# First up slab of a layer by token tile, from reused attention memory, and modulation sums in another order

## The chip, the core and the metric

The kernel runs on one core of a Trainium2 chip. The metric is the device time of one execution in microseconds; lower is better. All data is float32. TensorE runs at one of two clocks, and the profile gives the granted one as a share of 2.4 GHz.

## The reference, cut to what matters

Two blocks follow each other on 256 tokens of width 1024. The first has an even layer (Fourier mix and latent attention) and an odd layer (grouped attention), which also carry 256 context tokens. The second has two hybrid layers:

```python
u = layer_norm(x) * (1 + sc1) + sh1
proj = u @ w_in + b_in                # pool, conv, two attentions, 4 x 1024 gates
for n in range(4): merged += sigmoid(gate[n]) * (branch[n] @ w_branch[n])
x = layer_norm(ALPHA * x + g1 * (merged @ w_o)) * ln1_g + ln1_b
u2 = layer_norm(x) * (1 + sc2) + sh2
hdn = square(relu(u2 @ w_up + b_up))  # 1024 -> 4096
x = layer_norm(ALPHA * x + g2 * (hdn @ w_down)) * ln2_g + ln2_b
```

The shifts, scales and gates (`sh1`, `sc1`, `g1`, ...) are products of `silu(c)` with a 1024-wide matrix each, plus a bias.

## The kernel before

**Matmuls.** A float32 product at full precision is three products of parts: a weight slab (128 x 2048, 1 MB) is copied by ScalarE to a rounded high part (`high`, L1562, 1.9 us) and VectorE subtracts it from the slab for the low part (`low`, L2137, 2.3 us). The activations are split in the same way (`split_u`, L2449 and L2450). All matmuls are recorded at line 766, transposes at line 926.

**Slabs.** The SP queue loads the slabs in one fixed order, LAYER_SLABS, into `weight_ring` with three slots; a slab waits for its slot to be free. A slot comes free when VectorE has made the low part, or, for a `branch` slab, which is not split, when TensorE has used it. The high and low parts have two slots each; they come free when TensorE has used them. A gate tile of a hybrid layer takes two `gate` halves and one `branch` slab, so exactly the ring.

**Modulation.** A modulation vector is a weighted sum of matrix rows: POOL issues 1 MB chunks into `modulation_ring` (two slots, L638), VectorE adds each with a scalar (`gemv`, L1979, two instructions of 1.28 us for each stream; vectors 2 to 4 of the first block have two streams, latent and context, 5 and later one), and TensorE adds the 128 partial sums by a product with ones (`reduce_part`). Chunk q of vector c can be issued when VectorE has used the chunk two before it.

**Gate tile g of a hybrid layer.** TensorE: the features of gate g (96 matmuls of 256 columns), then branch g. ScalarE's queue: split of gate g+1, both halves, then tanh of gate g, which frees gate g's banks. These are the banks of gate g+1. VectorE: low parts of gate g+1, the products of gate and branch, then two chunks of gemv. POOL adds to `mergedT`.

**From the output projection to the MLP.** `o0` is computed for both token tiles at once, `o1` tile by tile. VectorE adds the residual and takes statistics (`halves_of_tile`, L2084 to L2091), centres and scales (`centred`, `scaled`, L2606 and L2612), takes statistics of the result (`statistics_again`) and writes the normalised tile `xn` (`normal`, L2120); POOL gives the inverse roots (L666). TensorE turns a tile of `xn` when it is ready (`turn_xn`) and computes the sums of vectors 1, 2 and 3 and some `keep_busy` matmuls between. ScalarE modulates the turned `xn` (L1838), VectorE splits it in four blocks, and only then does `up0` start, by features with all 256 tokens in each matmul (96 matmuls of 256 columns). `up0` is an ordinary slab of the ring. Then `up1`, `down0`, `up2` and so on.

**Memory.** Tensors share addresses by phase. Where the hybrid layer's attention keeps `qT`, `kT`, `v`, `prob` and where the pool matrices and forget sums lie, nothing is live from the fifth gate tile on; the last two of these places are those of the MLP's `hidden_high` and `hidden_low`.

**Even layer.** VectorE's order around the Fourier mix: split of `kva`, gemv (3,1), statistics of `qa` and `kva` with one `mgate` split between, the other `mgate` split, gemv (3,2), the four Fourier products (L2225), gemv (3,3), (4,0), (4,1), the gated tiles of `mgate`, rotations. TensorE's Fourier step g+1 (`f2`) writes the one bank that product g frees, and `mgate` follows step 3.

## Time and profile before

| what | value |
|---|---|
| median of 3 runs | 1394.52 us (1393.18 to 1396.90) |
| profiled execution | 1396.87 us, of it span 1395.10 |
| mean granted clock of TensorE | 0.983 |
| busy: TensorE, weight loads, VectorE, ScalarE, POOL | 94%, 78%, 68%, 36%, 11% |
| HBM read | 255.49 MB, 184 GB/s over the span |

Busy time says little by itself: TensorE's 94% count its filler matmuls too. What matters is where TensorE waits, for whom, and what that engine did before. Even and odd layer take the first 500 us or so, each hybrid layer some 450.

### The profile page before, as it was taken

Reading aid. Unit: us, or ns where it says so; the run is one execution under the profiler, and the core shown is the slowest. Engines: PE = TensorE matmul, PEld = TensorE weight load, DVE = VectorE, ACT = ScalarE, POOL = GpSimd, SP = SyncE. Lnnn points to the kernel's source line nnn. Section 1 sums busy time; section 2 is a strip of 40 time slices with the busy share of each in tenths; the row PEclk is TensorE's granted clock in tenths of the full one; section 3 lists DMA queues with packets and bytes.
Section 4 is the critical chain, followed back from the end, with each engine's and each line's share of the span. In section 5 each row is a group of like instructions: output and inputs, shape, how many; then the busy total and the mean of one; then the engine's idle time right before and its main releaser. Section 6 shows DMA issues by size and latency. Waiting matters only on the chain.

```text
span 1395.1 us, 19034 instructions
## 1 busy us (share of the span) xinstructions
PE 1314.8 (94%) x7923; PEld 1085.6 (78%) x7923; DVE 950.1 (68%) x1221; ACT 499.6 (36%) x769; POOL 151.3 (11%) x168
## 2 busy tenths in 40 slices
PE   5997999999999899999998999998999999999996
PEld 3796855446875459899887889886988998889895
DVE  4866667557488567577788666657667778755546
ACT  3321135214246023543323344323354333343432
POOL 2201100100000010012222000001001231100000
PEclk9998999999999999999999999999999999999998
DMA  9653360225420465577774777545656785455551
GB/s 358 232 178 108 138 211 1 95 87 183 157 100 1 153 214 184 197 257 270 273 286 142 235 245 246 182 151 181 200 187 247 260 299 199 136 192 186 181 181 61
DMA packets 104911, 257.77 MB, mean 185 GB/s; under 512 B 8213, under 2 KB 11766, under 8 KB 104570
## 3 DMA queue, kind: packets, MB, share of 16 engines
q1 hardware_dynamic: 80432, 171.75, 36.1%
q0 software_dynamic: 20192, 75.58, 15.0%
q10 hardware_dynamic: 4202, 9.23, 1.9%
q8 instruction: 63, 1.03, 0.3%
q14 instruction: 22, 0.18, 0.0%
HBM read 255.49 MB, written 1.05 MB: 184 GB/s over the span
## 4 chain that ended last, share of the span: by engine, by line
PE 70%; DVE 17%; DMA 4%; ACT 4%; issue 4%; POOL 1%; ACTq 0%; POOLq 0%; SPq 0%; DVEq 0%
PE bank L766 68%; DVE weights_low L2137 2%; PE bank L926 2%; DMA weight_ring<-in_w_in_dram 2%; DMA start_ring<-in_w_mod_dram 1%; DVE modulation_sums L1979 1%; ACT odd_prob L1751 1%; DVE statistics L2091 1%; POOL inverse_roots L666 1%; DVE negated_maxima L2381 1%; ACT weights_high L1562 1%; DMA modulation_ring<-in_w_mod_dram 1%; DMA modulation_ring<-in_w_ada_dram 1%; ACT even_A L1696 1%; DVE x L2090 1%
## 5 line engine op out<-in xcount | busy, mean ns | idle before, releaser
L2137 DVE TENSOR_TENSOR weights_low<-weight_ring,weights_high 128x2048 fp32r<-128x2048 f32 (+1 forms) x124 | 272.5, 2200 | 223.4 <-ACT weights_high L1562 223.3
L1562 ACT ACTIVATE weights_high<-weight_ring 128x2048 fp32r<-128x2048 f32 (+1 forms) x124 | 227.5, 1837 | 390.2 <-PE bank L766 315.5
L766 PE MATMUL bank<-uT_high,weights_high 128*128 128x256 f32 (+1 forms) x1200 | 342.0, 285 | 6.0 <-issue 2.7
L766 PE MATMUL bank<-uT_low,weights_high 128*128 128x256 f32 (+1 forms) x1200 | 340.1, 283 | 0.0
L766 PE MATMUL bank<-uT_high,weights_low 128*128 128x256 f32 (+1 forms) x1200 | 340.0, 283 | 0.0
L766 PEld LDWEIGHTS bank<-uT_high,weights_high 128*128 128x128 f32 (+1 forms) x1200 | 228.8, 191 | 11.3 <-ACT gate_tanh L1892 6.2
L766 PEld LDWEIGHTS bank<-uT_low,weights_high 128*128 128x128 f32 (+1 forms) x1200 | 228.9, 191 | 1.1
L766 PEld LDWEIGHTS bank<-uT_high,weights_low 128*128 128x128 f32 (+1 forms) x1200 | 228.8, 191 | 0.5
L1979 DVE SCALAR_TENSOR_TENSOR modulation_sums<-modulation_ring,silu_c_columns,modulation_sums 128x1024 f32<-128x1024 f32 x112 | 148.7, 1327 | 21.8 <-DMA modulation_sums<-in_b_ada_dram 7.1
L766 PE MATMUL bank<-weights_high,hidden_high 128*128 128x512 f32 x256 | 102.7, 401 | 1.2 <-DVE weights_low L2137 1.2
L766 PE MATMUL bank<-weights_low,hidden_high 128*128 128x512 f32 x256 | 102.0, 398 | 0.0
L766 PE MATMUL bank<-weights_high,hidden_low 128*128 128x512 f32 x256 | 102.0, 398 | 0.0
L638 POOL DMA_DIRECT2D modulation_ring<-in_w_ada_dram x48 | 34.7, 724 | 520.9 <-DVE modulation_sums L1979 511.0
L666 POOL TENSOR_TENSOR inverse_roots<-newton,inverse_roots 128x1 f32<-128x1 f32 (+1 forms) x25 | 25.6, 1023 | 412.7 <-DVE newton L2102 332.7
L766 PE MATMUL bank<-x,weight_ring 128*128 128x256 f32 x256 | 58.0, 380 | 2.0 <-issue 2.0
L766 PEld LDWEIGHTS bank<-weights_high,hidden_high 128*128 128x128 f32 x256 | 48.8, 191 | 12.5 <-issue 1.6
L766 PE MATMUL bank<-weight_ring,even_yT 128*128 128x512 f32 x128 | 55.7, 594 | 2.5 <-DVE even_yT L2279 1.4
L766 PEld LDWEIGHTS bank<-weights_high,hidden_low 128*128 128x128 f32 x256 | 48.6, 190 | 11.8
L766 PEld LDWEIGHTS bank<-weights_low,hidden_high 128*128 128x128 f32 x256 | 48.7, 190 | 10.9
L766 PE MATMUL bank<-weights_high,uT_high 128*128 128x256 f32 (+1 forms) x160 | 53.4, 334 | 1.8 <-DVE uT_low L2450 1.2
L766 PEld LDWEIGHTS bank<-x,weight_ring 128*128 128x128 f32 x256 | 47.5, 190 | 8.5 <-issue 2.8
L766 PE MATMUL bank<-weights_high,uT_low 128*128 128x256 f32 (+1 forms) x160 | 52.2, 327 | 0.0
(311 smaller groups left out, 2184.6 us busy)
## 6 DMA issues: line engine op xcount, KB each, us to landing
weight_ring<-in_w_in_dram SPq DMA_DIRECT2D x52, 1024.0 KB, 6.4
modulation_ring<-in_w_ada_dram POOLq DMA_DIRECT2D x48, 1024.0 KB, 6.9
weight_ring<-in_w_up_dram SPq DMA_DIRECT2D x32, 1024.0 KB, 5.4
weight_ring<-in_w_down_dram SPq DMA_DIRECT2D x32, 1024.0 KB, 4.9
modulation_ring<-in_w_mod_dram POOLq DMA_DIRECT2D x16, 1024.0 KB, 5.8
weight_ring<-in_o_w_in_dram SPq DMA_DIRECT2D x10, 1024.0 KB, 5.2
weight_ring<-in_w_branch_dram SPq DMA_DIRECT2D x16, 512.0 KB, 3.7
weight_ring<-in_w_o_dram SPq DMA_DIRECT2D x8, 1024.0 KB, 6.9
```

Source lines behind the costliest of these rows:

```text
L638: pool.dma_start(mring[:, slot, :].rearrange("p (k n) -> p k n", k=2), w.rearrange("(k p) n -> p k n", p=P)[:, 2 * q:2 * q + 2, c0:c0 + D] ...
L666: pool.tensor_tensor(root[:, 0, c:c + n], nwt[:, 0, c:c + n], root[:, 1, c:c + n], ALU.pow).then_inc(S["root_ready"], 1)
L766: return track(pe.matmul(*args, **kw))
L926: return track(pe.transpose(o, src, ident[0:rows, 0:rows]))
L1562: act.activation(ring[:, s, c0:kn * cols], wring[:, slot, c0:kn * cols], ACT.Copy).then_inc(S["high_ready"], 1)
L1696: ins = act.activation(prob_e[:, b, c0:c0 + n], src, ACT.Exp, bias=negmax[:, b, i:i + 1], accum_out=esum[:, b, i:i + 1])
L1751: ins = act.activation(oprob[:, b, j, i, :], o[:, :], ACT.Exp, bias=negmax[:, b, n:n + 1], accum_out=esum[:, b, n:n + 1])
L1979: ins = dve.scalar_tensor_tensor(out=a, in0=w[:, k, :], scalar=ccol[:, col:col + 1], in1=a, op0=ALU.mult, op1=ALU.add)
L2090: link(dve.scalar_tensor_tensor(out=xc, in0=xc, scalar=scale, in1=tmp, op0=ALU.mult, op1=ALU.add))
L2091: return dve.bn_stats(stat[:, i, 6 * h:6 * h + 6], xc)
L2137: dve.tensor_tensor(lo[:, s, c0:kn * cols], wring[:, slot, c0:kn * cols], hi[:, s, c0:kn * cols].bitcast(F32), ALU.subtract).then_inc(w_fr ...
L2381: ins = dve.tensor_reduce(m[:, i:i + 1], ready(("OS", p, i, j))[:, :], AX_X, ALU.max, negate=True)
```

## The change

It does three things. (a) `up0` leaves the ring's order. Its two halves are loaded by the SP queue ahead of `gate6` into memory that the attention no longer needs, are split there by ScalarE and VectorE in gate tiles 5 and 6 (`high_late`, `low_late`), the low part over the raw one. The other slabs move up in the ring. (b) `up0` is computed by token tile: the turned and modulated tile 0 is multiplied as soon as it is split (24 matmuls of 512 columns for each tile), each result is copied by ScalarE to `gate_tanh`'s memory, turned by TensorE (four transposes a tile) and goes on as before. VectorE's residual steps stand in another order for that, and the `keep_busy` calls between the modulation sums fall from ten to two. In layer 0 gemv (4,1) moves behind the split of `down0`. (c) On VectorE and POOL the gemv blocks of the first block stand in another order: (3,1) and (3,2) behind the Fourier products, (4,0) and (4,1) behind the first rotations, (5,0) and (5,1) behind the even attention, (6,0) and (6,1) behind the last `og` split.

```diff
                + [s for j in range(8) for s in halves(f"gate{j}") + [(f"branch{j}", 0)]]
-               + halves("o0", "o1", "up0") + [s for j in range(1, 8) for s in halves(f"up{j}", f"down{j - 1}")]
+               + halves("o0", "o1") + [s for j in range(1, 8) for s in halves(f"up{j}", f"down{j - 1}")]
...
-    jobs += mod_jobs(LAYER_MODS, 1, lo) + mod_jobs(LAYER_MODS, 2, lo)
-    jobs += [(("x2T", i), hi) for i in range(4)] + mod_jobs(LAYER_MODS, 3, lo)
+    jobs += mod_jobs(LAYER_MODS, 1, (4,)) + mod_jobs(LAYER_MODS, 2, (5,))
+    jobs += [(("x2T", t, b), (4 + 2 * t + b,)) for t in range(TC) for b in range(2)] + mod_jobs(LAYER_MODS, 3, lo)
+    jobs += [(("upt", t), (4 + t,)) for t in range(TC)]
...
                 for name, h in LAYER_SLABS:
+                    if (name, h) == ("gate6", 0):
+                        b, n = sec.bank(("PV", 3), 1)
+                        sp.wait_ge(free[b], n)
+                        for part in range(2):
+                            sp.dma_start(up_raw[part].rearrange("p (k n) -> p k n", k=4),
+                                         w_slab("up0", part, l)[0]).then_inc(late_in[part], 16)
...
-            mod_chunks(sec, 3)
+            mod_chunks(sec, 3, 0, 1)
             inverse_root(2, 0, TALL)
             inverse_root(3, 0, TALL)
+            mod_chunks(sec, 3, 2, 3)
             mod_part(sec, 4)
             mod_part(sec, 5)
             mod_chunks(sec, 6, 0, 1)
             mod_start(sec, 6)
-            mod_chunks(sec, 6, 2, 3)
             for i in range(TALL):
                 inverse_root(4 + i, i)
+            mod_chunks(sec, 6, 2, 3)
             mod_part(sec, 7)
 
...
+                if name == "up0":
+
+                    pe.wait_ge(S["late_low"], sec.at("late_low", h + 1))
+                    return [v.rearrange("p (k n) -> p k n", k=4) for v in up_parts[h]]
...
                 reduce_part(1)
-                keep_busy(start(("x2T", 0)), 3)
                 reduce_part(2)
-                keep_busy(start(("x2T", 0)), 3)
-                turn_xn("x2T", TC, between=lambda: reduce_part(3))
-                keep_busy(start(("up", 0, 0)), 4)
+                keep_busy(start(("x2T", 0, 0)), 2)
+                turn_tile(0, "x2T", TC)
+                reduce_part(3)
+                def up_of_tile(o, tt, ks):
+
+                    for k in ks:
+                        if k % 4 == 0:
+                            pe.wait_ge(S["u_ready"], sec.at("u_ready", 8 + 2 * tt + k // 4 + 1))
+                        ins = multiply(o[:, :], ui(k, tt), cut(slab("up0", k // 4), k % 4, 0, COLS),
+                                       start=(k == 0), stop=(k == KD - 1))
+                    if KD - 1 in ks:
+                        done(ins, ("upt", tt))
+
+                def turn_up(outs, tt):
+
+                    copied(("upt", tt))
+                    for i, o in enumerate(outs):
+                        for m in range(2):
+                            ins = turn(o[:, N * m + P * tt:N * m + P * tt + P],
+                                       tanhg[:, tt, P * (2 * i + m):P * (2 * i + m) + P], P)
+                        if tt == TC - 1:
+                            done(ins, ("up", 0, i))
+
+                o = start(("upt", 0))
+                up_of_tile(o, 0, range(6))
+                turn_tile(1, "x2T", TC)
+                up_of_tile(o, 0, range(6, KD))
+                o = start(("upt", 1))
+                up_of_tile(o, 1, range(4))
+                firsts_up = [start(("up", 0, i)) for i in range(2)]
+                turn_up(firsts_up, 0)
+                up_of_tile(o, 1, range(4, KD))
+
+                def finish_first(k):
+
+                    if k == 3:
+                        turn_up(firsts_up, 1)
+
                 for j in range(9):
-                    if j < 8:
+                    if 1 <= j < 8:
                         features_out(both(f"up{j}"), [("up", j, 0), ("up", j, 1)], u, N, 2,
-                                     wait=u_split(2) if j == 0 else lambda k: None)
+                                     wait=finish_first if j == 1 else lambda k: None)
                     if j == 8 and not sec.last:
...
 
+                def high_late(h):
+
+                    act.wait_ge(late_in[h], l * 16 + 16)
...
                                 ins = act.activation(prob[:, j, c:c + n], o[:, c:c + n], ACT.Exp,
                                                      bias=negmax[:, j, i:i + 1], accum_out=esum[:, j, i:i + 1])
                             release(ins, ("S", g, j))
+                    if g in (5, 6):
+                        high_late(g - 5)
                     if g < 7:
                         high(f"gate{g + 1}")
                         gate_tanh(g)
...
-                high("o1", "up0")
-
+                high("o1", "up1")
+                copied(("mod", 1))
+                copied(("mod", 2))
+                modulate_tile("x2T", 0, mcol2)
+                copied(("o", 1, 1))
+                gate_rows(3, [grow1])
                 act.wait_ge(S["norm1"], sec.at("norm1", 1))
                 load_norm(l, 2)
-                copied(("mod", 1))
-                copied(("mod", 2))
-                modulate_u("x2T", mcol2)
-                gate_rows(3, [grow1])
+                modulate_tile("x2T", 1, mcol2)
+                for tt in range(TC):
+                    copy_out(("upt", tt), tanhg[:, tt, :], ready(("upt", tt))[:, :])
                 for j in range(8):
-                    high(f"down{j - 1}" if j > 0 else "up1")
+                    if j > 0:
+                        high(f"down{j - 1}")
...
             low_e("kva", 1)
-            gemv(3, 1)
 
...
             low_e("mgate", 1)
-            gemv(3, 2)
             copied(("f0",))
...
                 release(ins, ("f2", g))
-            gemv(3, 3)
+            for q in range(1, 4):
+                gemv(3, q)
             mod_columns(2, mcol, 0)
-            for q in range(2):
-                gemv(4, q)
             for m in range(4):
                 gated_tile(("mgate", m), 4 + m, eyT[:, 4 + m, :], tanh_e[:, m % 2, :])
...
                 link(rotate(src, src, cos16[:, i, :], sin16[:, i, :], 1, 16, ps))
+            for q in range(2):
+                gemv(4, q)
             for h in range(2):
...
             ins.then_inc(S["kpe_ready"], 1)
             for q in range(2, 4):
                 gemv(4, q)
-            for q in range(2):
-                gemv(5, q)
             for h in range(MH):
...
-            for q in range(2, 4):
+            for q in range(4):
                 gemv(5, q)
-            for q in range(2):
-                gemv(6, q)
             for v in range(2):
                 copied(("mod", 4, v, 1))
...
             low("og1")
-            for q in range(2, 4):
+            for q in range(4):
                 gemv(6, q)
...
+                def low_late(h):
+
+                    hi, lo = up_parts[h]
+                    dve.wait_ge(S["late_high"], sec.at("late_high", h + 1))
+                    dve.tensor_tensor(lo, up_raw[h], hi.bitcast(F32), ALU.subtract).then_inc(S["late_low"], 1)
...
+                    if g in (5, 6):
+                        low_late(g - 5)
                     if g < 7:
                         low(f"gate{g + 1}")
...
-                low("o1")
+                low("o1", 0)
...
                 def residual_of_mixed(m):
 
+                    link(halves_of_tile("o", 1, 0))
                     link(halves_of_tile("o", 0, 1))
                     variance(0, False, LN_EPS)
                     centred(0)
-                    link(halves_of_tile("o", 1, 1))
-                    variance(1, False, LN_EPS)
                     link(scaled(0, m))
                     statistics_again(0)
-                    centred(1)
-                    normal(0, m + 2)
-                    scaled(1, m + 1).then_inc(S["norm1"], 1)
-                    dve.wait_ge(S["norm1"], sec.at("norm1", 1))
-                    statistics_again(1)
+                    link(halves_of_tile("o", 1, 1))
                     mod_columns(1, mcol2, 0)
                     mod_columns(2, mcol2, 1)
+                    normal(0, m + 1)
+                    variance(1, False, LN_EPS)
+                    centred(1)
+                    scaled(1, m + 2).then_inc(S["norm1"], 1)
+                    dve.wait_ge(S["norm1"], sec.at("norm1", 1))
+                    split_block("x2T", 0, 0)
+                    statistics_again(1)
+                    split_block("x2T", 0, 1)
                     normal(1, m + 3)
 
...
-                for i in range(TC):
-                    link(halves_of_tile("o", i, 0))
+                link(halves_of_tile("o", 0, 0))
+                low("o1", 1)
                 dve.wait_ge(ln_in, l * 64 + 32)
                 residual_of_mixed(1)
-                low("up0", 0)
-                for i in range(4):
-                    copied(("x2T", i))
-                    split_u(i)
-                low("up0", 1)
+                for b in range(2):
+                    split_block("x2T", 1, b)
+                low("up1")
                 for j in range(8):
-                    if not sec.last:
+                    if not sec.last and j != 1:
                         gemv(4 + j // 4, j % 4)
-                    low(f"down{j - 1}" if j > 0 else "up1")
+                    if j > 0:
+                        low(f"down{j - 1}")
+                    if not sec.last and j == 1:
+                        gemv(4, 1)
                     copied(("up", j, 1))
```

`split_block` is the split of four 128 x 128 blocks of one token tile; `copied` waits until a bank is free, `link` for the instruction just issued. `modulate_tile` is the former loop over `xT` with a name, and `turn_tile` the former one of the same name.

## Rows read from the trace of the kernel before

**Rows 1.** the page's chain that ended last, share of the span by engine
```profile
PE 70%; DVE 17%; DMA 4%; ACT 4%; issue 4%; POOL 1%; ACTq 0%; POOLq 0%; SPq 0%; DVEq 0%
```
**Rows 2.** TensorE's timeline, even layer: start, us, instruction, [idle before <- releaser]
```profile
112.21 0.36 PE L766 MATMUL bank<-even_C,even_constants 128*128 128x8 f32 x2 [1.09 <-DVE even_E L2215]
128.68 4.45 PE L766 MATMUL bank<-even_constants,even_C 128*128 128x256 f32 x16 [6.49 <-DVE even_yT L2225]
136.32 1.97 PE L766 MATMUL bank<-even_constants,even_C 128*128 128x256 f32 x8 [1.06 <-DVE even_yT L2225]
...
203.81 0.64 PE L926 MATMUL bank<-constants,even_B 128*96 128x128 f32 x4 [0.49 <-DVE even_E L2263]
```
**Rows 3.** VectorE's timeline in the same stretch, columns as in Rows 2
```profile
106.06 0.57 DVE L2003 BATCH_NORM_STATS2 statistics<-bank 128x6 f32<-128x384 f32 x1
122.62 1.28 DVE L1979 SCALAR_TENSOR_TENSOR modulation_sums<-modulation_ring,silu_c_columns,modulation_sums 128x1024 f32<-128x1024 f32 x1
```
**Rows 4.** windows: length, PE, PEld, DVE, ACT, POOL busy, granted clock, DMA share, GB/s
```profile
128.00:132.00 4.00, 3.32 (x8) 2.70 (x9) 0.53 (x2) 0.00 (x0) 1.78 (x3) 0.51 0.00 0
164.00:168.00 4.00, 4.00 (x19) 3.54 (x20) 1.53 (x14) 1.47 (x3) 1.46 (x2) 0.50 0.28 113
```
**Rows 5.** odd layer, VectorE, then TensorE; landings of chunks issued at 264.4, 267.1
```profile
385.74 5.24 DVE L1979 SCALAR_TENSOR_TENSOR modulation_sums<-modulation_ring,silu_c_columns,modulation_sums 128x1024 f32<-128x1024 f32 x4
394.23 0.68 DVE L2372 COPY odd_kT<-bank 128x512 f32<-128x512 f32 x1
...
395.12 1.99 PE L766 MATMUL bank<-odd_kT,odd_qT 64*128 64x512 f32 x8 [1.36 <-issue]
...
DMA to landing us min/median/max: 5.6/5.6/5.6
...
DMA to landing us min/median/max: 6.5/6.5/6.5
```
**Rows 6.** layer 0, gates 5 and 6: chain of waits, then ScalarE, then TensorE
```profile
665.75 11.68 DMA weight_ring<-in_w_in_dram
...
671.60 1.92 ACT L1562 ACTIVATE weights_high<-weight_ring 128x2048 fp32r<-128x2048 f32 x1 [7.27 <-DMA weight_ring<-in_w_in_dram]
677.45 1.92 ACT L1562 ACTIVATE weights_high<-weight_ring 128x2048 fp32r<-128x2048 f32 x1 [3.92 <-DMA weight_ring<-in_w_in_dram]
...
680.91 0.36 PE L766 MATMUL bank<-uT_high,weights_high 128*128 128x256 f32 x1 [1.27 <-ACT gate_tanh L1892]
```
**Rows 7.** SP queue, landings (branch 5, gate 6, layer 1), one window
```profile
665.23 1.02 SPq L596 DMA_DIRECT2D weight_ring<-in_w_in_dram  x2
...
DMA to landing us min/median/max: 3.6/3.6/3.6
...
DMA to landing us min/median/max: 6.3/9.0/11.7
...
DMA to landing us min/median/max: 6.7/8.6/10.6
...
674.00:678.00 4.00, 4.00 (x29) 3.77 (x28) 1.92 (x1) 0.56 (x1) 0.32 (x1) 1.00 1.03 410
```
**Rows 8.** TensorE's timeline, layer 0, from output projection to MLP
```profile
734.70 1.84 PE L766 MATMUL bank<-constants,modulation_sums 128*128 128x1 f32 x16
...
743.73 1.06 PE L926 MATMUL bank<-constants,xn 128*128 128x128 f32 x8 [2.70 <-DVE xn L2120]
748.66 1.09 PE L926 MATMUL bank<-constants,xn 128*128 128x128 f32 x8 [2.15 <-DVE xn L2120]
...
752.50 0.77 PE L766 MATMUL bank<-uT_high,weights_high 128*128 128x256 f32 x1
...
777.25 0.47 PE L766 MATMUL bank<-weights_high,hidden_high 128*128 128x512 f32 x1 [1.06 <-DVE weights_low L2137]
```
**Rows 9.** VectorE's timeline in the same stretch
```profile
731.74 0.69 DVE L2084 TENSOR_TENSOR xn<-bank,gate_row 128x512 f32<-128x512 f32 x1
...
742.77 0.81 DVE L2120 TENSOR_SCALAR xn<-x,mean_variance,inverse_roots 128x1024 f32<-128x1024 f32 x1 [0.52 <-POOL inverse_roots L666]
```

80 lines of the change are left out of this document (38 added, 42 removed).

## The prediction

> **What bounds the kernel now.** I read the page first: TensorE carries 70% of the chain that ended last [rows 1]. So time is won or lost only where TensorE stands still, runs at its lower clock, or does filler matmuls. Next I read TensorE's timeline at the three places that the change touches; the reader is to see there how long the idle time is and what ended it. They are the last stretch of the even layer's Fourier mix (6.49 us) [rows 2], the hand-over from the output projection to the MLP in each hybrid layer [rows 8, 9], and, as a place that is full today, the gate tiles [rows 6]. Last come the queues beside them: VectorE [rows 3, 5], ScalarE and the SP queue [rows 6, 7].
>
> **Even layer, the gain.** Two gemv blocks (4 instructions of 1.28 us, 5.0 us a block) leave VectorE's path to the Fourier products: one before the statistics of `qa`, one after the last `mgate` split [rows 3]. Without the first, statistics start at 101.1 instead of 106.06 and `qa`'s banks are free near 107.6, so `f0` follows `kva` directly: its 1.09 us wait goes [rows 2], some 1.2 with the restart. TensorE then reaches the point of the long wait at 122.18 - 1.2 = 121.0. The `kva` statistics wait for `kva`'s last tile (111.1) and end with a root near 113.5; the copies and the last split end near 117.9, so VectorE's first product is out before 121.0 and the 6.49 us wait is gone. From 128.68 to `mgate`'s start at 137.94 it is 9.26 us today; 1.35 of them are the first product at the lower clock, which the idle time had brought (0.51 of full) [rows 2, 4]. So `mgate` starts at 121.0 + 7.9 = 128.9, 9.0 us earlier. gemv (3,1) to (3,3) then run 130 to 147, beside `mgate` (96 matmuls of 512 columns, some 22.5 us), and end before their sum is wanted at 151. Given back: gemv (4,0) and (4,1), 10.0 us, now stand ahead of the `qb` rotations (157.6 to 167.6), and the second half of `qb` needs those banks: 170.1 against 169.2, 0.9 us. Won: the 0.49 us wait in the key transposes, as gemv (5,0), (5,1) have left that place [rows 2]. Sum **-8.5 us**. It holds through the even attention, where no gemv stands. The four blocks of gate 1's sum behind the attention cost nothing: the output tiles, which come next on VectorE, end later on TensorE. On POOL the latents' roots now go ahead of chunks (3,2) and (3,3), as the second needs gemv (3,1), and those of the odd norm ahead of (6,2); none waits for more than before.
>
> **Odd layer, the price.** gemv (6,0) and (6,1) move behind the last `og` split, so four blocks stand where two stand: today 5.24 us from 385.74, then the four gated tiles and the key copy, which ends at 394.91 and lets the first score matmul go at 395.12 [rows 5]. The move costs more than two blocks of 2.62. The ring has two slots, so POOL can issue chunk (6,2) only when gemv (6,0) has ended: 385.74 + 2.62 + 0.3 = 388.65, and a chunk lands 5.6 us after its issue, its follower 6.5 [rows 5]. gemv (6,2) runs 394.3 to 396.9; (6,3), issued at 391.3, lands at 397.8 and ends at 400.4. Gated tiles and key copy start 9.4 us later than at 391.02, and I take +9.0 for the scores. TensorE stands idle some 8 us, and 6.49 us was enough to bring the lower clock (1.2 of 2.4 GHz) and keep it for 3.3 us of the restart, 128.68 to 132 [rows 2, 4]; half of that, **+1.7**, comes on top. Sum **+10.7**. The blocks can't slide forward: they stand behind the last split, which ends as they begin.
>
> **Hybrid layers, the price.** Three gate slabs fill the three ring slots, so a branch load waits until TensorE has used the last branch, and the SP queue issues branch 5, gate 6 half 0 and half 1 in one burst from 664.82 to 666.25 [rows 7]. ScalarE waits for both halves, 7.27 and 3.92 us [rows 6], and its queue has `high("gate6")` before `gate_tanh(5)`, and the tanh frees the banks that gate 6 needs. The chain of waits runs through that very load (11.68 us) [rows 6]. The change issues `up0`'s two megabytes between branch 5 and gate 6: the wait written there (PV 3's bank) was met at 656, so it delays nothing and protects nothing. Within the SP queue loads land in turn (3.6, 6.3, 11.7 us after issue) [rows 7]. 2.10 MB at the 410 GB/s that both queues move there [rows 7] are 5.1 us; at the rate between branch 5's and half 0's landing, 1.05 MB in 3.15 us, they are 6.3; and the SP queue shares with a modulation chunk for longer. I take +6.4: gate 6's half 1 lands near 683.8, is split 1.92 us, tanh, and TensorE starts 3.5 us after the landing as now, at 687.3 against 680.91 [rows 6]. In layer 1 the half lands 10.6 us after its issue at 1116.0 [rows 7], at 1126.6, just as TensorE frees the buffer, so 1133.0 + 3.5 against 1130.45 without a wait for it: +6.1. I take **+6.25** a layer; the lower end is 3.7 (5.1 less the 1.4 us for which the last modulation chunk may give way), the upper 7.7. Below zero is excluded, as no load gets earlier. TensorE idles 6.6 to 7.7 us, so **+1.7** for the lower clock, as above. ScalarE's extra 1.92 and VectorE's 2.29 us in gates 5 and 6 lie in their waits for the same loads, and cost nothing while those last; without them VectorE has about 1 us to spare in a gate tile. A rule of the Trainium skill bears on this step. The page "DMA: Bandwidth & Descriptors", section "Where 436 GB/s comes from", has transfers from HBM bound at about 358 GB/s; the trace here shows more, 410, so the measurement decides. By the page the two megabytes would take 5.9 us and the layer would lose half a microsecond less; the sum does not use it.
>
> **Hybrid layers, the gain.** Today: `o1` ends and the sums follow at 734.70, residual and statistics of tile 0 on VectorE, turn of tile 0 at 743.73, tile 1 at 748.66, `up0` at 752.50, and `up0` with `up1` (192 matmuls) ends at 776.19 [rows 8]. In the new order VectorE takes tile 1's half 0 at 727.4, tile 0's half 1 at 729.6 (2.2 us earlier), and tile 0's scaling and statistics before tile 1's last half [rows 9]; normal 0 starts at 739.3 against 742.77. (The terms: tile 1's last half 2.2 us as today, POOL's root 1.5, a scaling 1.3, statistics 1.8.) `u` of tile 0's first four blocks is ready near 744.8. Each tile has 24 matmuls of 512 columns, at 0.23 us, twice the 0.12 of today's 192 of 256 columns: 18 of them run before tile 1 is turned (749.5), the rest after, and tile 1's split on VectorE (1.1 us a block) is ready at 752.1 and 753.2. ScalarE's copies of the two sums lie beside TensorE's next blocks. Tile 1 ends at 758.0. Then `up1`, with four transposes in it (0.5 us), ends at 770.2: 6.0 us earlier. The next wait, 1.06 us for a split of `down0` [rows 8], grows to about 1.4, since gemv (4,1) now follows that split. Layer 1 is faster today by 1.1 us (normal 1 took 0.81, not 1.41), so 5.2 there. Two waits inside are short of filler now: only two `keep_busy` calls remain of ten, and the sums of one column each bring the lower clock by themselves [rows 4]; I take 0.6 off. **-4.9** a layer, bounds -3.5 (lower clock throughout `up0`'s first 18 matmuls) and -5.8.
>
> **The sum.** Even -8.5, odd +10.7, two layers of +6.25 + 1.7 - 4.9 = +3.05, so +6.1: together **+8.3 us**. Against the profiled execution, 1396.87 (span 1395.10 and 1.77 around it), that is 1405.2; the median of the runs is 1394.52, so I forecast **1402.8**.
>
> **Rivals.** (1) *The collision is covered*: gate 6's loads land as before, because the DMA engines take them beside `up0` and what stands behind gives way, and the layers keep only their gain: 2 x -4.9 + 2.2 = -7.6, 1386.9. For it: no row shows more than three loads waiting in this queue. Against: the landings in it come in turn [rows 7], and `up0` stands ahead. It decides from the point where half 1 lands before 677. (2) *Half collision*: the stall is 3 us a layer and too short for much of the lower clock (0.8): 2 x -1.1 + 2.2 = 0, 1394.5. (3) *The odd layer's wait is smaller*, chunks landing early: half of 10.7 gone, 1397.5; the landings of 5.6 and 6.5 us speak against it. (4) *The change doesn't do what it says*: `up0` by tile starts at the lower clock and later, saving 1.5 a layer: 8.3 + 6.8 = 1409.6. For it: the idle steps without filler.
>
> **How the numbers follow.** Forecast 0.55 (its own range 1397 to 1409), (1) 0.16, (2) 0.12, (3) 0.1, (4) 0.07. The range reaches from 1388 to 1409: above (1)'s centre, where less than 0.15 is left out, and up to the bounds of the stalls. A measurement of this kernel can tell about 0.3% (4.2 us) from no change. Faster than 1390.3: (1) and a tail of (2), 0.19. Within: the rest of (2), (3)'s lower half, 0.21. Slower: 0.60.
>
> **What would show it.** In the profile after: the score matmuls of the odd layer start after an idle time of about 8 us on TensorE (1.36 before), with POOL's chunk landing ahead of a gemv. Gate 6 starts after a wait of 7 us or so for `gate_tanh`, in both layers, with ScalarE waiting for the weight ring. `mgate` starts near 129. `up1` ends 35.5 us after `o1` in layer 0, against 41.5. The forecast is wrong if gate 6 starts within 2 us of branch 5's end, if VectorE does not wait between gemv (6,1) and (6,2), or if the Fourier stage keeps a wait of over 3 us.

## The result, and the profile of the changed kernel

| kernel | median | ratio to before, 95% interval | span of the profiled execution | mean granted clock |
|---|---|---|---|---|
| before | 1394.19 us (1393.18 to 1396.90, 4 runs) | | 1395.1 us | 0.983 |
| after | 1409.54 us (1408.66 to 1411.22, 4 runs) | 1.0108 [1.0094, 1.0122] | 1409.4 us | 0.976 |

Ratios are taken against executions of the kernel before made beside each run, whose medians were 1394.2 to 1395.3 us; one execution of e6 (3308.79 us) and one of the kernel before (3321.88 us) are left out of them.

The change costs 15.4 us by the medians and 14.3 us in the two profiled spans. The forecast had the sign right and the size wrong: 8.3 us, 1402.8, and the time lies above the range's end of 1409. The page of the changed kernel: its span, the granted clock in tenths over 40 slices, and the engines' shares of the chain that ended last. Before, that chain held 4% of DMA [rows 1]; now it holds 7%.

```profile
span 1409.4 us, 18841 instructions
...
PEclk9999999999989999999899999999999989999999
...
PE 69%; DVE 14%; DMA 7%; ACT 4%; issue 4%; POOL 1%; ACTq 1%; SPq 0%; POOLq 0%; DVEq 0%
```

To find where the time went, take TensorE's timeline in both kernels, note when the same matmul starts, and subtract. Each stage's own cost is the step from one line to the next.

| TensorE starts | before | after | later by | forecast |
|---|---|---|---|---|
| even output projection | 259.92 | 250.71 | -9.2 | -8.5 |
| odd scores | 395.12 | 394.91 | -0.2 | +0.5 |
| hybrid layer 0 | 500.88 | 502.14 | +1.3 | +2.2 |
| layer 0, branch 5 | 676.02 | 677.89 | +1.9 | +2.2 |
| layer 0, gate 6 | 680.91 | 690.71 | +9.8 | +8.5 |
| layer 0, branch 6 | 692.50 | 705.00 | +12.5 | +10.2 |
| layer 0, sums behind `o1` | 734.70 | 747.31 | +12.6 | +10.2 |
| layer 0, `up2` | 788.51 | 797.01 | +8.5 | +5.3 |
| hybrid layer 1 | 950.23 | 956.06 | +5.8 | +5.3 |
| layer 1, branch 5 | 1126.30 | 1133.43 | +7.1 | +5.3 |
| layer 1, gate 6 | 1130.45 | 1146.06 | +15.6 | +11.5 |
| layer 1, branch 6 | 1142.04 | 1159.74 | +17.7 | +13.2 |
| layer 1, sums behind `o1` | 1184.26 | 1202.22 | +18.0 | +13.2 |
| layer 1, `down0` | 1224.34 | 1238.68 | +14.3 | +8.3 |

**Even layer.** TensorE's timeline in the Fourier stage after: the 6.49 us wait of [rows 2] is gone, the short one before the last step stays. `mgate` starts at 127.78 for 137.94, 10.2 us earlier, though the kernel after is 1.0 us late from 42 us on (the same matmul at 42.70 for 41.68), which nothing in the change touches. The second half of `qb` starts at 167.97 for 178.20, still 10.2 us earlier, but after a wait of 2.34 us (0.78 before) that VectorE's rotations end. Behind it the clock is lower, 0.60 from 168 to 172 us, and 1.0 us of the gain is gone by the output projection.

```profile
123.14 1.97 PE L787 MATMUL bank<-even_constants,even_C 128*128 128x256 f32 x8 [0.17 <-DVE even_yT L2275]
126.16 1.97 PE L787 MATMUL bank<-even_constants,even_C 128*128 128x256 f32 x8 [1.06 <-DVE even_yT L2275]
127.78 0.58 PE L787 MATMUL bank<-even_hT_high,even_weights_high 128*128 128x512 f32 x1
```

**Odd layer.** VectorE behind the last `og` split, POOL's two issues, then TensorE, where [rows 5] had 5.24 us of gemv and 1.36 us idle. After (6,0) and (6,1) VectorE waits 4.18 us for a chunk that POOL could issue only at 379.39. TensorE stands 8.39 us, and its eight score matmuls take 3.79 us where they took 1.99.

```profile
376.50 5.24 DVE L2031 SCALAR_TENSOR_TENSOR modulation_sums<-modulation_ring,silu_c_columns,modulation_sums 128x1024 f32<-128x1024 f32 x4
385.92 5.25 DVE L2031 SCALAR_TENSOR_TENSOR modulation_sums<-modulation_ring,silu_c_columns,modulation_sums 128x1024 f32<-128x1024 f32 x4 [4.18 <-DMA modulation_ring<-in_w_ada_dram]
...
379.39 0.73 POOL L658 DMA_DIRECT2D modulation_ring<-in_w_ada_dram  x1 [66.24 <-DVE modulation_sums L2031]
...
392.04 1.09 PE L951 MATMUL bank<-constants,odd_q 128*128 128x128 f32 x4 [8.39 <-DVE odd_yT L2119]
394.91 3.79 PE L787 MATMUL bank<-odd_kT,odd_qT 64*128 64x512 f32 x8 [0.94 <-issue]
```

**Gate 6, layer 0.** The SP queue's burst, ScalarE's splits, TensorE in both layers, and windows whose last three columns are the granted clock, the DMA engines' share and GB/s. Against [rows 6] half 1 is split 9.8 us later (687.23 for 677.45), and TensorE waits 9.20 us for 1.27.

```profile
666.69 0.37 SPq L610 DMA_DIRECT2D weight_ring<-in_w_branch_dram  x1
667.10 0.47 SPq L626 DMA_DIRECT2D hidden_raw<-in_w_up_dram  x1
667.61 0.51 SPq L626 DMA_DIRECT2D late_raw<-in_w_up_dram  x1
668.17 1.99 SPq L610 DMA_DIRECT2D weight_ring<-in_w_in_dram  x2
...
684.61 1.91 ACT L1608 ACTIVATE weights_high<-weight_ring 128x2048 fp32r<-128x2048 f32 x1 [9.48 <-DMA weight_ring<-in_w_in_dram]
687.23 1.92 ACT L1608 ACTIVATE weights_high<-weight_ring 128x2048 fp32r<-128x2048 f32 x1 [0.71 <-DMA weight_ring<-in_w_in_dram]
...
690.71 0.55 PE L787 MATMUL bank<-uT_high,weights_high 128*128 128x256 f32 x1 [9.20 <-ACT gate_tanh L1933]
1146.06 0.55 PE L787 MATMUL bank<-uT_high,weights_high 128*128 128x256 f32 x1 [9.02 <-ACT gate_tanh L1933]
...
680.00:684.00 4.00, 1.51 (x7) 0.97 (x6) 0.00 (x0) 0.00 (x0) 0.00 (x0) 1.00 1.03 403
684.00:688.00 4.00, 0.00 (x0) 0.00 (x0) 1.45 (x1) 2.68 (x2) 0.00 (x0) 0.83 0.43 158
688.00:692.00 4.00, 1.29 (x6) 1.32 (x7) 3.66 (x4) 4.00 (x6) 0.00 (x0) 0.50 0.00 0
692.00:696.00 4.00, 4.00 (x21) 4.00 (x21) 3.96 (x4) 0.41 (x1) 3.49 (x2) 0.50 0.79 265
```

**From `o1` to the MLP, layer 0.** TensorE's sums and the first waits behind them, then VectorE around `up2`. The two idle times of 2.70 and 2.15 us in [rows 8] are gone; 0.87, 0.69 and 0.99 us stand there now. But `up2` waits 2.17 us for its low part, as gemv (4,1) and the steps on `up1`'s result stand between the splits of `down0` and `up2`.

```profile
747.31 3.63 PE L787 MATMUL bank<-constants,modulation_sums 128*128 128x1 f32 x32
751.80 2.07 PE L787 MATMUL bank<-constants 128*128 128x256 f32 x4 [0.87 <-DVE modulation_columns L2066]
757.72 0.47 PE L787 MATMUL bank<-hidden_high,uT_high 128*128 128x512 f32 x1 [0.69 <-issue]
765.43 0.47 PE L787 MATMUL bank<-hidden_high,uT_high 128*128 128x512 f32 x1 [0.99 <-issue]
797.01 0.36 PE L787 MATMUL bank<-uT_high,weights_high 128*128 128x256 f32 x1 [2.17 <-DVE weights_low L2189]
...
788.14 2.60 DVE L2031 SCALAR_TENSOR_TENSOR modulation_sums<-modulation_ring,silu_c_columns,modulation_sums 128x1024 f32<-128x1024 f32 x2
794.58 4.59 DVE L2189 TENSOR_TENSOR weights_low<-weight_ring,weights_high 128x2048 fp32r<-128x2048 f32 x2
```

### The profile page after: what moved, and what is told of

It is laid out like the page before. It is cut to its first block, busy times and chain, and to the rows that moved or that the text cites. A ratio compares the mean times of both kernels' runs of the same rounds, so it can differ in the third digit from the quotient of the medians.

```text
span 1409.4 us, 18841 instructions
## 1 busy us (share of the span) xinstructions
PE 1313.2 (93%) x7811; PEld 1077.5 (76%) x7811; DVE 951.7 (68%) x1221; ACT 507.2 (36%) x789; POOL 149.0 (11%) x168
## 4 chain that ended last, share of the span: by engine, by line
PE 69%; DVE 14%; DMA 7%; ACT 4%; issue 4%; POOL 1%; ACTq 1%; SPq 0%; POOLq 0%; DVEq 0%
PE bank L787 67%; DMA weight_ring<-in_w_in_dram 4%; PE bank L951 2%; DVE weights_low L2189 2%; DVE modulation_sums L2031 1%; DMA start_ring<-in_w_mod_dram 1%; DMA modulation_ring<-in_w_ada_dram 1%; ACT weights_high L1608 1%; ACT odd_prob L1797 1%; DVE negated_maxima L2428 1%; DVE statistics L2143 1%; ACT even_A L1742 1%; DVE even_A L2128 1%; POOL inverse_roots L686 1%; DMA weight_ring<-in_w_o_dram 1%
## 5 line engine op out<-in xcount | busy, mean ns | idle before, releaser
L2189 DVE TENSOR_TENSOR weights_low<-weight_ring,weights_high 128x2048 fp32r<-128x2048 f32 (+1 forms) x120 | 263.1, 2197 | 229.6 <-ACT weights_high L1608 229.6
L1608 ACT ACTIVATE weights_high<-weight_ring 128x2048 fp32r<-128x2048 f32 (+1 forms) x120 | 220.0, 1835 | 377.3 <-PE bank L787 304.1
L787 PE MATMUL bank<-uT_high,weights_high 128*128 128x256 f32 (+1 forms) x1136 | 325.4, 286 | 25.5 <-ACT gate_tanh L1933 18.2
L787 PE MATMUL bank<-uT_low,weights_high 128*128 128x256 f32 (+1 forms) x1136 | 323.4, 285 | 0.0
L787 PE MATMUL bank<-uT_high,weights_low 128*128 128x256 f32 (+1 forms) x1136 | 323.3, 285 | 0.0
L787 PEld LDWEIGHTS bank<-uT_high,weights_high 128*128 128x128 f32 (+1 forms) x1136 | 218.4, 192 | 30.9 <-ACT gate_tanh L1933 22.7
L787 PEld LDWEIGHTS bank<-uT_low,weights_high 128*128 128x128 f32 (+1 forms) x1136 | 218.5, 192 | 1.1
L787 PEld LDWEIGHTS bank<-uT_high,weights_low 128*128 128x128 f32 (+1 forms) x1136 | 218.3, 192 | 0.5
L2031 DVE SCALAR_TENSOR_TENSOR modulation_sums<-modulation_ring,silu_c_columns,modulation_sums 128x1024 f32<-128x1024 f32 x112 | 148.7, 1327 | 18.8 <-DMA modulation_ring<-in_w_ada_dram 11.1
L787 PEld LDWEIGHTS bank<-weights_high,hidden_high 128*128 128x128 f32 x256 | 48.1, 188 | 11.6 <-issue 0.7
L787 PEld LDWEIGHTS bank<-weights_high,hidden_low 128*128 128x128 f32 x256 | 48.1, 188 | 11.7
L787 PEld LDWEIGHTS bank<-weights_low,hidden_high 128*128 128x128 f32 x256 | 48.1, 188 | 10.8
L1866 ACT ACTIVATE mergedT<-bank,modulation_columns 128x128 f32<-128x128 f32 x64 | 23.3, 473 | 84.5 <-PE bank L951 84.5
```

The costliest lines, as they stand in the source:

```text
L787: return track(pe.matmul(*args, **kw))
L1608: act.activation(ring[:, s, c0:kn * cols], wring[:, slot, c0:kn * cols], ACT.Copy).then_inc(S["high_ready"], 1)
L1866: ins = act.activation(whole[:, k, P * tt:P * tt + P], o[:, P * n:P * n + P], ACT.Identity, bias=cols[:, 0, k:k + 1], scale=cols[:, 1, k:k ...
L2031: ins = dve.scalar_tensor_tensor(out=a, in0=w[:, k, :], scalar=ccol[:, col:col + 1], in1=a, op0=ALU.mult, op1=ALU.add)
L2189: dve.tensor_tensor(lo[:, s, c0:kn * cols], wring[:, slot, c0:kn * cols], hi[:, s, c0:kn * cols].bitcast(F32), ALU.subtract).then_inc(w_fr ...
```

## The experiments

The theory behind all of them is the table above: the loss sits in gate 6 of both layers, and even and odd layer cancel. Three things were open. Is gate 6's wait one of bytes on the DMA engines, or of the new splits in ScalarE's queue? Does the odd wait belong to the place of two blocks, so that moving them back wins it? And what bounds the gain of the new order?

### e1, e2, e3: the modulation sums

**e1**: before, with part (c) of the change alone.

> The kernel before with the new order of the modulation sums in the even and the odd layer alone, without any change in the hybrid layers. Theory: the ledger of the two traces holds term by term. The even layer's mgate starts near 128.0 and the first eout matmul near 250.7 (9.2 us earlier), the odd score matmuls start near 394.9 after 8.4 us idle on TensorE, restart at the lower clock, and the first hybrid layer starts 1.3 us later than in the kernel before. Time 1395.5 us, ratio 1.001. Rival: the hybrid layers' new order takes part in the even and odd figures (other slot numbers of the weight ring), then the two stages move by more than 2 us against the kernel after.

Measured 1395.14 us, ratio 1.0004 [0.9991, 1.0018]. So (c) as a whole costs nothing that can be measured, and the whole loss comes from (a) and (b): 14.4 us by the medians, where the forecast had 6.1. The trace has the ledger's steps, 7.95 us idle ahead of the odd scores among them, but 2 us shifted: output projection at 248.61, odd scores at 392.40, hybrid layer 0 at 500.01, which is 2.1, 2.5 and 2.1 us earlier than in the kernel after. That is past the 2 us which the expectation set as the mark of its rival. 1.0 us of it stands there at 42 us already, ahead of anything that was changed, and another 1.0 arises by 192 us, where the clock of after was 0.60 (168 to 172 us) and that of e1 was 1.00. So the shift looks like chance of the clock, but this run does not exclude the rival.

**e2**: as e1, but (6,0), (6,1) stay in the output stage. **e3**: the kernel after with the same two blocks moved back; the cut is e3's.

```diff
             for q in range(4):
                 gemv(5, q)
+            for q in range(2):
+                gemv(6, q)
...
             low("og1")
-            for q in range(4):
+            for q in range(2, 4):
                 gemv(6, q)
```

> The kernel before with the new order in the even layer alone; blocks (6,0) and (6,1) stay in the even output stage, so that six blocks stand there in place of four. Theory: the Fourier stage gains 9.2 us and nothing gives it back, as the odd layer's wait came from the four blocks behind og alone: 1385 us, ratio 0.9934, odd score matmuls after 1.4 us idle. Rival: the two blocks more in the output stage (5.2 us of VectorE) delay the residual and the odd norm, and some 4 us of the gain go there: 1389 to 1390.

> The kernel after with blocks (6,0) and (6,1) back in the even output stage, nothing else changed. Theory: the 8.4 us idle before the odd score matmuls and the 1.8 us of lower clock behind it go, and the hybrid layers keep their shape: 1399.1 us, 10.5 below the kernel after, ratio 1.0035 to the kernel before. Rival: what is won is taken again further on (the first hybrid layer's loads bound it), then less than 6 us come.

Measured 1393.32 us, 0.9995 [0.9982, 1.0008] for e2, and 1407.71, 1.0096 [1.0075, 1.0116] for e3: 9 us were expected of the one, 10.5 of the other, and both gave under 2. The rivals hold in that the gain is taken again further on, and more strongly than written; the place, ahead of `eout`'s second half, is the one that e2's rival named. The odd wait is gone in both, and a new one of the same size stands ahead of the second half of `eout`. VectorE's and TensorE's rows of e2, then TensorE's of e3:

```profile
274.92 5.25 DVE L1980 SCALAR_TENSOR_TENSOR modulation_sums<-modulation_ring,silu_c_columns,modulation_sums 128x1024 f32<-128x1024 f32 x4 [8.99 <-DMA modulation_sums<-in_b_ada_dram]
...
287.71 15.38 PE L767 MATMUL bank<-weight_ring,even_yT 128*128 128x512 f32 x32 [9.47 <-DVE dulation_sums_of_context L2085]
```

```profile
285.32 4.92 PE L787 MATMUL bank<-weight_ring,even_yT 128*128 128x512 f32 x7 [9.13 <-DVE dulation_sums_of_context L2136]
```

Six blocks in a stage that had four is the same fault as four where two stood. With two ring slots only the first two blocks find their chunks landed; every pair beyond waits until POOL has issued and the DMA has brought what it needs, here 3.14 us for the second pair and 8.99 us for the third (last of all the bias row of vector 6, issued behind the chunks). The kernel before has one such wait in this stage, 7.10 us, and TensorE's output projection covers it; two it does not cover, and VectorE's residual steps stand behind them. The two blocks too many come from (5,0) and (5,1), which left the key transposes.

**e9** puts just these back: (5,0), (5,1) ahead of the key copies, (5,2) to (6,1) in the output stage, (6,2), (6,3) behind `og`, all as before; only vectors 3 and 4 keep the new order, in the kernel before. The cut is against e2.

```diff
             for q in range(2, 4):
                 gemv(4, q)
+            for q in range(2):
+                gemv(5, q)
             for h in range(MH):
...
-            for q in range(4):
+            for q in range(2, 4):
                 gemv(5, q)
```

> The kernel before with the new order only for the blocks of sums 3 and 4 in the even layer; blocks (5,0) and (5,1) stay ahead of the key copies, (6,0) and (6,1) in the output stage, as in the kernel before. Theory from e2 (there the two blocks more in the output stage made the sums wait for their chunks, 9.5 us idle before the second half of eout): with the old distribution of blocks over the stages, the 9 us of the Fourier stage are kept; the key copies wait about 1 us for block (5,1). First hybrid layer 8 to 9 us earlier than before, time 1386.5 us, ratio 0.994. Rival: some chunk wait behind the attention takes most of it again whatever the distribution, since the row of modulation sums is bound by its own two slots and not by TensorE: 1392 or more.

Measured **1384.23 us** (1381.93 to 1385.15), 0.9918 [0.9903, 0.9934]. The rival falls: the even layer's gain holds through the whole kernel. The output projection starts at 249.01, 10.9 us earlier than before, and the odd scores at 384.31, 10.8 us earlier, after the same 1.36 us idle; of the waits over 1.4 us behind the Fourier stage only the one ahead of `qb`'s second half is longer (2.14 for 0.78 us). The first hybrid layer starts 13.0 us earlier, but some 2 of these are the clock, 0.57 from 456 to 460 us before and 1.00 at the same work in e9, behind the same idle time (2.13 and 2.12 us).

### e4, e6, e10: what gate 6 waits for

**e4**: loads as in after, splits of `up0` behind the tanh and the products of gates 5 and 6.

```diff
-                    if g in (5, 6):
-                        high_late(g - 5)
                     if g < 7:
                         high(f"gate{g + 1}")
                         gate_tanh(g)
+                        if g in (5, 6):
+                            high_late(g - 5)
```

> The kernel after, with the loads of up0 as they are, but ScalarE's and VectorE's splits of up0 behind gate_tanh and the products of gates 5 and 6 in place of ahead of gate 6's and gate 7's splits. Theory (the loads stand in the way): gate 6 still starts after 9 us idle on TensorE in both layers, the time is 1409.5 us within 2 us. Rival (the splits stand in the way on ScalarE or VectorE): the idle time before gate 6 falls by 2 to 4 us in each layer, 1402 to 1405 us.

Measured 1408.80 us, 1.0096 [1.0065, 1.0126]. TensorE waits as long as in after, and ScalarE now stands idle for 18.21 us until gate 6's first half lands. The splits' place is not the cause.

```profile
680.50 1.91 ACT L1608 ACTIVATE weights_high<-weight_ring 128x2048 fp32r<-128x2048 f32 x1 [18.21 <-DMA weight_ring<-in_w_in_dram]
...
686.60 0.56 PE L787 MATMUL bank<-uT_high,weights_high 128*128 128x256 f32 x1 [9.01 <-ACT gate_tanh L1933]
```

**e6**: only one of `up0`'s two megabytes ahead of gate 6, the other right behind it.

> The kernel after with only one of the two megabytes of up0 ahead of gate 6 in the SP queue, the other right behind gate 6's halves. Theory (the wait is a matter of bytes in one queue): one megabyte less at 410 GB/s is 2.6 us, so gate 6 starts after about 6.5 us idle in place of 9.2 (layer 0) and 9.0 (layer 1), with a similar lower clock behind it: 1404 us. If a modulation chunk no longer lands ahead of gate 6's half 1, up to 2.6 us more in each layer: 1399. Rival (ScalarE's order, or a wait for an event and not bytes): the idle time stays near 9 us, 1409.

**e10**: the kernel after, with chunk (3,1) issued behind POOL's additions for branch 5 instead of branch 4.

```diff
-                    if j == 4:
-                        mod_chunks(sec, 3, 1)
                     if j == 5:
+                        mod_chunks(sec, 3, 1)
                         mod_chunks(sec, 3, 2, 3)
```

> The kernel after with one modulation chunk, (3,1), issued behind POOL's additions for branch 5 in place of branch 4, so that one chunk less is in flight when up0 and gate 6 are loaded. Theory (gate 6's half 1 lands only when that chunk, too, has nearly landed): the idle time before gate 6 falls by 2.0 to 2.6 us from 9.2 and 9.0 us; behind gate 6 VectorE waits for the late chunk, so the whole time says little (1405 to 1415). Rival (the chunk gives way to the SP queue): idle time unchanged within 0.5 us.

e6: 1405.40 us, 1.0073 [1.0049, 1.0096]; e10: 1414.12 us, 1.0135 [1.0112, 1.0158] from two executions. e10 is slower as a whole: gate 7 now waits 3.91 and 3.07 us for its low parts, which stand behind the late chunk on VectorE (0.55 in the kernel after), and in layer 0 its 96 matmuls then took 13.1 us for 11.6; the rest of the 4.6 us is not taken apart. TensorE before gate 6 of layer 0, first in e6, then in e10:

```profile
685.31 0.55 PE L788 MATMUL bank<-uT_high,weights_high 128*128 128x256 f32 x1 [6.33 <-ACT gate_tanh L1934]
```

```profile
687.64 0.55 PE L786 MATMUL bank<-uT_high,weights_high 128*128 128x256 f32 x1 [6.70 <-ACT gate_tanh L1932]
```

A megabyte of `up0` less takes 2.9 us off the wait, a megabyte of modulation chunk less 2.5 us, though the chunk goes by another queue (layer 1: 3.3 and 3.3, from 9.02 to 5.69 and 5.77). So what is behind in the SP queue waits for POOL's bytes too, and e10's rival, a chunk that gives way, is out. The Trainium skill has the rule, page "DMA: Bandwidth & Descriptors", section "Queues, rings and completion order": each DMA engine takes packets in turn from the queues that have work for it. The two runs agree with it.

### e5, e7, e8: the loads elsewhere

**e5**: both loads behind gate 6's halves, splits one gate step later. **e7**: first load behind gate 6's halves, second behind gate 7's, splits behind tanh and products as in e4. `UP0_AT` tells ahead of which slab each half is issued: both ahead of `branch6` in e5, half 0 ahead of `branch6` and half 1 ahead of `branch7` in e7.

```diff
-                    if (name, h) == ("gate6", 0):
+                    if (name, h) in UP0_AT:
                         b, n = sec.bank(("PV", 3), 1)
                         sp.wait_ge(free[b], n)
-                        for part in range(2):
+                        for part in UP0_AT[name, h]:
```

> The kernel after with the two loads of up0 behind gate 6's halves in the SP queue, ahead of branch 6, and their splits one gate step later. Theory (collision of the loads): gate 6 starts 1.3 us after branch 5 in layer 0 and 0.5 us in layer 1 as in the kernel before, and the lower clock behind it goes: 21 us less than the kernel after, 1388 us, ratio 0.996. Rival 1 (the collision only moves): up0's two megabytes now delay gate 7, whose burst has no room either, and 2 to 5 us a layer stay there: 1392 to 1398. Rival 2 (the wait for PV 3's bank or the splits were the cause): nothing comes back, over 1405.

> The kernel after with up0's first load behind gate 6's halves and its second behind gate 7's, each split behind the tanh and the products of the gate step. Theory: neither gate 6 nor gate 7 waits for its weights, 1388 us, and if e5 shows a wait before gate 7, this one is faster by it. Rival: the loads for o0 are delayed in turn and TensorE waits some 2 us before the output projection in each layer: 1392.

e5: 1395.11 us, 0.9997 [0.9984, 1.0011]; e7: 1391.32 us, 0.9972 [0.9955, 0.9990]. Gates 6 and 7 of layer 0 in e5, then in e7:

```profile
679.65 0.36 PE L788 MATMUL bank<-uT_high,weights_high 128*128 128x256 f32 x1 [0.65 <-issue]
697.72 0.42 PE L788 MATMUL bank<-uT_high,weights_high 128*128 128x256 f32 x1 [2.87 <-ACT gate_tanh L1934]
```

```profile
680.27 0.36 PE L788 MATMUL bank<-uT_high,weights_high 128*128 128x256 f32 x1 [1.10 <-ACT gate_tanh L1934]
696.02 0.35 PE L788 MATMUL bank<-uT_high,weights_high 128*128 128x256 f32 x1 [0.55 <-issue]
```

In e5 14.4 us of the loss come back and a part moves to gate 7 (2.87 us here, 2.77 in layer 1), as its first rival had it. With one megabyte in each gap (e7) neither gate waits longer than in the kernel before, and another 3.8 us come. e7 had 1388 expected and missed it by 3: the forecast for it took no account of `up2`'s wait. Its rival's number, 1392, is nearer, but its mechanism is there in small only: the output projection waits 1.29 us in both layers in place of 0.62, and for a split of VectorE (`uT_low`), not for a load.

**e8**: e5 and e3 together.

> e5 and e3 together: up0's loads behind gate 6, and blocks (6,0), (6,1) back in the even output stage. Theory: all terms add up, 1388 less 10.5 = 1378 us, ratio 0.988 to the kernel before. Rival: the faster front part brings the lower clock or a load wait elsewhere, 1382 or more.

Measured 1392.75 us, 0.9998 [0.9984, 1.0011]: 15 us short of the theory. e5 itself had come out 7 us above its 1388, and of e3's 10.5 us no more than 1.8 exist; by the ratios e8 can't be told from e5 (0.9997).

### e11, e12: the wait before `up2`, and all together

**e11**: e7 with gemv (4,1) behind the split of `up2`.

```diff
-                    if not sec.last and j == 1:
-                        gemv(4, 1)
                     copied(("up", j, 1))
...
                     if j > 0:
                         low(f"up{j + 1}" if j < 7 else "down7")
+                    if not sec.last and j == 1:
+                        gemv(4, 1)
```

> e7 with block (4,1) of the modulation sums behind the split of up2 in place of between the splits of down0 and up2, in the first hybrid layer. Theory (the 2.17 us idle before up2 is VectorE's row of splits with that block in it, and it brings the lower clock in part of the executions): the wait goes, 2 to 3.5 us less than e7, 1388. Rival (up2's load or ScalarE's split is what comes last): no change, 1391.

Measured 1387.86 us, 0.9943 [0.9925, 0.9960], 3.5 us below e7: the upper end of what was expected. No idle time is left before `up2` in its trace, so the rival is out. The size is less sure than the mechanism: e11's four executions (1386.17 to 1388.91) lie within the ten of e7 (1386.05 to 1395.78), and the two intervals overlap.

**e12**: e7, e9 and e11 together.

> e7, e9 and e11 together: up0 by token tile with its loads behind gate 6 and gate 7, blocks of sums 3 and 4 in the new order with 5 and 6 at their old places, block (4,1) behind the split of up2. Theory: the even layer's 9 us, the MLP's 5 a layer and the wait before up2 add up to 1394.8 - 8.5 - 6 (e7's layers) - 2.5 = 1378 us, ratio 0.988 to the kernel before. Rival: the stages are coupled by loads and clock so that a third is lost, 1384.

Measured **1378.56 us** (1376.94 to 1381.46), 0.9882 [0.9865, 0.9900], with 1378 forecast. That is 1.2% less than the kernel before and 31 us less than the kernel after. That the sum came out to half a microsecond is in part luck: its terms were 8.5 and 8.5 us, while e9 and e11 alone are 11.1 and 7.5 us below the kernel before, and of these 18.6 us together 16.8 came. The odd scores start after 1.36 us again, and gate 6 after 0.80:

```profile
387.14 1.99 PE L788 MATMUL bank<-odd_kT,odd_qT 64*128 64x512 f32 x8 [1.36 <-issue]
672.52 0.36 PE L788 MATMUL bank<-uT_high,weights_high 128*128 128x256 f32 x1 [0.80 <-ACT gate_tanh L1934]
```

## Why the prediction was wrong in size

**Even layer, right.** -8.5 forecast, -9.2 in the trace of after, by the mechanism named (-11.3 in e1 and -10.9 in e9, so one profile is good for 2 us here). What `qb` was to give back, 0.9 us by a later start of its second half, came another way: that half starts 10.2 us earlier, as `mgate` does, and 1.0 us goes behind it, at the lower clock. One sentence of that part was wrong in what it left out: that (5,0) and (5,1) leave the key transposes was booked as 0.49 us won. They were the two blocks too many of the stages behind (e2, e3 against e9).

**Odd layer, right.** +10.7 forecast; +10.5 from the even output projection to the first hybrid layer. Its steps came as written: the late issue, the chunk landing in VectorE's row, about 8 us idle, the lower clock behind it. The rival of a smaller wait is out. What the forecast did not see is that the price is not tied to the place: moved back, the blocks cost the same elsewhere.

**Gate 6's wait, right in kind, mis-sized: the first step that failed.** 6.25 us a layer were taken, with 7.7 as the upper bound; the trace has 7.9 (9.80 less 1.87) and 8.5 (15.61 less 7.13). The term took 6.4 us for `up0`'s 2.1 MB, near the rate between two landings, and had half 1 land ahead of part of the chunks, as it did before: in the kernel before the windows show 4.2 MB moved from branch 5's issue to half 1's landing, of 4.7 in flight. After, the windows from 668 to 688 hold 6.8 MB, which is branch 5, `up0`, gate 6 and both modulation chunks entire. So 2.6 MB more had to pass, not 2.1, which is 6.7 us at some 390 GB/s. The other 1.2 us lie at the end: before, the engines still moved some 400 GB/s when half 1 had landed (677.45); after, they fell to 262, 160, 49 and 12 GB/s in the half microseconds from 685.0 to 687.0, and half 1 was there at 687.2. Why it took that long is not shown. e10 shows the chunk's share by itself. Both layers: +3.9 us.

**The lower clock, mis-sized: the second.** +1.7 a stall had been scaled from the restart after 6.49 us [rows 2, 4]. Gate 6's 96 matmuls and the start of branch 6 came 2.7 and 2.1 us later than its first matmul explains, with the clock at 0.50 to 696, five us behind the restart, where the forecast had counted on 3.3 us at the lower clock. The odd scores lost 1.8. Both layers: +1.4 us.

**The way to the MLP, right in kind, mis-sized: the third.** 35.5 us from `o1`'s end to `up1`'s end were forecast for layer 0; it is 36.2 (747.47 to 783.64), against 41.3. That miss is the 0.99 us wait for tile 1's split: from tile 1's turn (762.00) ScalarE's modulation and VectorE's first split took 3.3 us, where the forecast had 2.6. From the first matmul behind it (765.43) to `up1`'s end it is 18.2 us for 18.1. But the next wait was said to grow to 1.4 us at `down0`. That one went; 2.17 us came at `up2`, one slab further down VectorE's row. Net of it layer 0 keeps 4.1 us by `up2`, and layer 1, which has no gemv there, 3.6 us, where -4.9 each stood in the sum. About +2.5 us with what is lost in the next slabs; e11 takes the wait out, and is 3.5 us below e7.

**Not in the sum.** Hybrid layer 1 begins with a wait of 1.25 us for a low part that the trace of before does not have at that place, +1.3, and layer 0 with 0.6 more. Against it the end of layer 0's MLP went 3.2 us faster than before, by the clock alone (below): that is luck of the one profile. 3.9 + 1.4 + 2.5 less 1.3 for these and 0.9 for even and odd layer make 5.6 of the 6.0 us between the forecast 8.3 and the measured 14.3 of the spans; the other 0.4 lies between branch 6 and the end of `o1` in the two layers.

**The rivals.** The covered collision (1386.9) and the half collision (1394.5) are out by the wait of 9.20 us. What they describe came near in e5 (a wait of 2.87 us, ahead of gate 7) and in e7 (none), where the loads stand behind the gate, and then came 1395.11 and 1391.32. The rival at 1409.6, nearest by its number, is not what happened: `up0` by tile does save most of what was said (5.1 us of 6.0 by `up1`'s end in layer 0).

**The range.** By its own bounds, 7.7 for the stall and -3.5 for the way to the MLP, the two layers add 5.7 us to 1402.8, which is about the upper end. Nothing was left for the lower clock, which had no bound, nor for a wait that is not in the sum. Measured, the stall lay past its bound in both layers (7.9, 8.5), the way came within 0.6 and 0.1 us of its own (-4.1, -3.6), and the clock added 1.4 us: three misses of one sign in the same two layers.

## What to carry to other kernels

Before moving a load ahead in a queue, count all bytes in flight at that point on every queue, and read what the last consumer waits for: here it landed when nearly all of them had passed. Spread what has to be added over the gaps between bursts, a megabyte in each here. And with a ring of two slots, count the consumers in each stage, not only their instructions: two found their data landed here, each pair beyond waited for an issue and a landing (3.14 to 8.99 us), and the stage must have other work to cover that.

## What the runs showed of the hardware

**The clock falls by chance at the same place.** At the end of layer 0's MLP 32 one-column matmuls stand ahead of 48 of 512 columns in both kernels. TensorE before, with the windows behind it, and then TensorE after with its windows:

```profile
925.05 4.84 PE L766 MATMUL bank<-constants,modulation_sums 128*128 128x1 f32 x32
...
925.00:929.00 4.00, 4.00 (x30) 3.96 (x29) 2.36 (x2) 2.01 (x2) 0.00 (x0) 0.78 0.83 262
929.00:933.00 4.00, 4.00 (x13) 3.33 (x13) 0.00 (x0) 0.00 (x0) 0.00 (x0) 0.50 0.79 242
```

```profile
934.03 3.63 PE L787 MATMUL bank<-constants,modulation_sums 128*128 128x1 f32 x32
...
934.00:938.00 4.00, 4.00 (x35) 3.92 (x34) 2.36 (x2) 2.01 (x2) 0.00 (x0) 1.00 0.81 265
938.00:942.00 4.00, 4.00 (x19) 3.23 (x18) 1.26 (x2) 0.00 (x0) 0.00 (x0) 1.00 0.78 254
```

The first lost 3.2 us to the lower of the two clocks, the second nothing. The first is the rule: in thirteen of the fourteen profiles here the 48 matmuls took 12.8 to 14.1 us, and only in after 11.3. So the profiled spans of before and after lie some 3 us closer together at this place than usual. The idle 2.17 us before `up2` brought the lower clock in five of the eight profiles that have it (e3, e4, e5, e6 and e10, where `up2`'s 96 matmuls took 13.2 us) and not in after, e7 and e8 (11.7 us). The Trainium skill, page "TensorE: Matmul & The Clock Gate", section "What's actually happening", says of a kernel's start that the number of slow matmuls differs between runs of one kernel; the rows here show the like in the middle of kernels that are alike at that place. In a kernel of 1400 us with several such places single profiles can differ by some 3 us with no cause in the program. The ten executions of e8, one and the same kernel, go from 1389.18 us at a mean granted clock of 0.986 to 1397.50 at 0.979, and the profiled one is the fastest of them; the median is 1392.75.

**The DMA engines of one core moved 386 to 412 GB/s** over windows of 4 us with two queues at work (386 to 407 in after from 672 to 684 us, 412 in before from 672 to 676 us), and 2.5 to 3.3 us is what a megabyte adds to the wait of the last load behind it.
